# Gate tiles of the second block: the product with the root on VectorE, straight from PSUM

## The reference, cut to what matters

```python
h = rms_norm(x, norm_mix_g[layer])
z = h @ w_in[layer]
y_a = hgrn2_mixer(...)              # from columns of z
y_b = forgetting_attention(...)     # from columns of z
gate_a = jax.nn.sigmoid(z[..., OFF_GATE:OFF_GATE + D_MODEL])
gate_b = jax.nn.sigmoid(z[..., OFF_GATE + D_MODEL:IN_COLS])
merged = gate_a * (y_a @ w_branch_a[layer]) + gate_b * (y_b @ w_branch_b[layer])
x = x + merged @ w_out[layer]
```

## Time and profile before

| | us |
|---|---|
| three timed runs | 1060.25, 1057.53, 1059.84 |
| their median | 1059.84 |
| profiled execution | 1060.18 |
| its span, first to last instruction | 1058.4 |
| TensorE busy | 992.4 (94%) |
| VectorE busy | 702.0 (66%) |
| ScalarE busy | 532.7 (50%) |
| GpSimd busy | 65.6 (6%) |
| mean granted TensorE clock | 0.956 of full |

### The profile page before, as it was taken

One profiled execution on the slowest core, in us unless ns is written; L12 is line 12 of the kernel. 1 busy time (PEld: TensorE's weight loads), 2 busy tenths in 40 slices (PEclk: granted clock), 3 DMA queues, 4 the chain that ended last, 5 costly groups with the idle time before them and its releaser, 6 DMA issues.

```text
span 1058.4 us, 15667 instructions
## 1 busy us (share of the span) xinstructions
PE 992.4 (94%) x6699; PEld 912.0 (86%) x6699; DVE 702.0 (66%) x810; ACT 532.7 (50%) x641; POOL 65.6 (6%) x73
## 2 busy tenths in 40 slices
PE   5999889999978979999999899998999999999988
PEld 4998888989878968989998788898798999999976
DVE  5876693434957487878887659979437555455463
ACT  4555611224474644767776654365354543434352
POOL 3000330410000100000000000002000000000000
PEclk9999997897979879999999999999999999999989
DMA  7655301002224325979999144434235466555521
GB/s 221 218 179 159 96 25 41 1 2 80 81 80 149 129 80 185 356 291 348 360 362 351 53 159 160 125 122 145 87 120 171 159 200 203 193 191 169 199 80 41
DMA packets 91195, 168.54 MB, mean 159 GB/s; under 512 B 6268, under 2 KB 61941, under 8 KB 86262
## 3 DMA queue, kind: packets, MB, share of 16 engines
q1 hardware_dynamic: 90374, 167.22, 46.0%
q10 hardware_dynamic: 752, 0.33, 0.1%
HBM read 166.48 MB, written 1.05 MB: 158 GB/s over the span
## 4 chain that ended last, share of the span: by engine, by line
PE 70%; DVE 15%; ACT 9%; issue 4%; DMA 0%; ACTq 0%; DVEq 0%
PE ps L1004 8%; PE ps L1007 7%; PE ps L1006 7%; PE ps L1022 7%; PE ps L1023 7%; PE ps L1024 7%; DVE w_lo L1740 5%; ACT w_hi L518 4%; PE ps L1394 3%; PE ps L1395 3%; PE ps L1396 3%; PE ps L1218 2%; PE ps L1231 2%; PE ps L1227 2%; PE ps L1434 1%
## 5 line engine op out<-in xcount | busy, mean ns | idle before, releaser
L1740 DVE TENSOR_TENSOR w_lo<-raw,w_hi 128x2048 fp32r<-128x2048 f32 (+1 forms) x158 | 365.6, 2318 | 167.2 <-ACT w_hi L518 166.1
L518 ACT ACTIVATE w_hi<-raw 128x2048 fp32r<-128x2048 f32 (+1 forms) x158 | 299.9, 1902 | 80.6 <-PE ps L1024 63.2
L1004 PE MATMUL ps<-h_hi,w_hi 128*128 128x256 f32 x768 | 222.0, 289 | 3.2 <-DVE h_lo L1750 2.1
L1007 PE MATMUL ps<-h_hi,w_lo 128*128 128x256 f32 x768 | 219.8, 286 | 0.0
L1006 PE MATMUL ps<-h_lo,w_hi 128*128 128x256 f32 x768 | 219.8, 286 | 0.0
L1004 PEld LDWEIGHTS ps<-h_hi,w_hi 128*128 128x128 f32 x768 | 150.2, 196 | 5.3 <-issue 3.5
L1006 PEld LDWEIGHTS ps<-h_lo,w_hi 128*128 128x128 f32 x768 | 150.2, 196 | 0.4
L1007 PEld LDWEIGHTS ps<-h_hi,w_lo 128*128 128x128 f32 x768 | 149.9, 195 | 0.0
L1022 PE MATMUL ps<-w_hi,h_hi 128*128 128x512 f32 (+1 forms) x240 | 95.1, 396 | 2.5 <-DVE h_lo L2094 2.1
L1023 PE MATMUL ps<-w_lo,h_hi 128*128 128x512 f32 (+1 forms) x240 | 93.5, 390 | 0.0
L1024 PE MATMUL ps<-w_hi,h_lo 128*128 128x512 f32 (+1 forms) x240 | 93.1, 388 | 0.0
(11 more groups left out here) (454 smaller groups left out, 1595.9 us busy)
## 6 DMA issues: line engine op xcount, KB each, us to landing
raw<-in_w_in SPq DMA_DIRECT2D x36, 1024.0 KB, 5.1
raw<-in_w_exp_gate SPq DMA_DIRECT2D x20, 1024.0 KB, 5.2
raw<-in_w_exp_up SPq DMA_DIRECT2D x20, 1024.0 KB, 4.9
raw<-in_w_exp_down SPq DMA_DIRECT2D x20, 1024.0 KB, 5.1
raw<-in_w_ffn_gate SPq DMA_DIRECT2D x11, 1024.0 KB, 5.2
raw<-in_w_ffn_up SPq DMA_DIRECT2D x11, 1024.0 KB, 5.3
raw<-in_w_ffn_down SPq DMA_DIRECT2D x11, 1024.0 KB, 4.8
raw<-in_w_out SPq DMA_DIRECT2D x8, 1024.0 KB, 5.0
```

The costliest lines, as they stand in the source:

```text
L518: act.activation(w_hi[:, j % SPL, 0:kt * n], raw[:, j % RAW, 0:kt * n], ACT.Copy).then_inc(w_high, 1)
L1004: pe.matmul(o, hi[:, k, cols], a_hi[:, k, :], start=(k == 0 and (whole or c == 0)), stop=False)
L1007: last_mm = pe.matmul(o, lo[:, k, cols], a_hi[:, k, :], start=False, stop=(k == kt - 1 and (whole or c == len(outs) - 1)))
L1740: dve.tensor_tensor(w_lo[:, j % SPL, 0:kt * n], raw[:, j % RAW, 0:kt * n], w_hi[:, j % SPL, 0:kt * n].bitcast(F32), sub).then_inc(w_ready, 1)
```

## The change

ScalarE no longer copies the gate tiles of the second block and GpSimd no longer multiplies them. VectorE multiplies each tile by `root_rep` as it reads it from the bank, writes it into `gate2` and raises `s_gate_ev2`. ScalarE's sigmoid waits for that semaphore at 8; `s_gate_sc` is gone. ScalarE's `ahead` calls stay where they were, without the copies. TensorE's program is unchanged. The eight products are placed in VectorE's order behind the low parts named in the diff; the second one stands in the middle of `o_norm`. (`gate_out` stays for the first block.)

```diff
@@ gpsimd
-            pool.wait_ge(s_rrep, 1)
-            for c in range(8):
-                pool.wait_ge(s_gate_ev2, c + 1)
-                g = gate2[:, 2 * c:2 * c + 2, :]
-                pool.tensor_tensor(g, g, mid(root_rep, 2), ALU.mult).then_inc(s_gate_sc, 1)
@@ scalar
-            gate_out(GATE2, 0, gate2, s_gate_ev2)
+            ahead(GATE2[1])
             act.wait_ge(s_hg_ps, 3)
             act.activation(ho, split3(bank(2, 2), 2), ACT.Copy).then_inc(s_hg_ev, 1)
-            gate_out(GATE2, 1, gate2, s_gate_ev2)
+            ahead(GATE2[2])
...
-            gate_out(GATE2, 2, gate2, s_gate_ev2)
+            ahead(GATE2[3])
             out_high(1, 2)
-            gate_out(GATE2, 3, gate2, s_gate_ev2)
-            gate_out(GATE2, 4, gate2, s_gate_ev2)
+            ahead(GATE2[4])
+            ahead(GATE2[5])
...
-            gate_out(GATE2, 5, gate2, s_gate_ev2)
-            gate_out(GATE2, 6, gate2, s_gate_ev2)
+            ahead(GATE2[6])
+            ahead(GATE2[7])
             prob_tiles(prob2_t, 6)
-            gate_out(GATE2, 7, gate2, s_gate_ev2)
...
-            act.wait_ge(s_gate_sc, 8)
+            act.wait_ge(s_gate_ev2, 8)
@@ vector
+            def gate_scaled(c):
+
+                dve.wait_ge(w_used, GATE2[c] + 1)
+                dve.tensor_tensor(gate2[:, 2 * c:2 * c + 2, :], split3(bank(6 + c % 2), 2), mid(root_rep, 2),
+                                  mult).then_inc(s_gate_ev2, 1)
...
             ahead(GATE2[1])
+            gate_scaled(0)
+            def gate_two():
+                ahead(GATE2[2])
+                gate_scaled(1)
+
             o_norm(ho, hsq, 1, HG_HEADS, HG_D, rep[:, C_ONORM:C_ONORM + HG_D], z2[:, :, Z2_G:Z2_G + 512],
-                   lambda: ahead(GATE2[2]))
+                   gate_two)
...
             ahead(GATE2[3])
+            gate_scaled(2)
             out_low(1, 2)
             ahead(GATE2[4])
+            gate_scaled(3)
             ahead(GATE2[5])
+            gate_scaled(4)
             softmax(prob2, ...
             ahead(GATE2[6])
+            gate_scaled(5)
             ahead(GATE2[7])
+            gate_scaled(6)
             ahead(PROJ2[0][0])
+            gate_scaled(7)
             attention_low(1)
```

More of the change, by code:

```diff
@@ L352, in two_block_program @@
             "first_half_of_down_in_psum", "root_diagonal_ready", "root_rows_in_psum", "root_rows_ready"))
-        s_scaled, s_gate_sc, s_ple_half = (sem(n) for n in (
-            "scaled_by_root", "gate_scaled_by_root", "ple_tile_in_psum"))
+        s_scaled, s_ple_half = (sem(n) for n in (
+            "scaled_by_root", "ple_tile_in_psum"))
         SQUARES = (2, 4, 4, 4, 4, 4)
```

## The result

The change made the kernel slower by a third of a percent. Twelve runs have a median of 1062.25 us, twelve of the kernel before 1058.01; the ratio is 1.0033, 95% interval 1.002 to 1.0047, about +3.5 us. A second comparison on the chip gave 1.0036 (1.0017 to 1.0055). The profiled execution has a span of 1059.6 us.

A forecast was written before the change was run, and what follows sets the result against it. VectorE was taken to bound the chain before 730.3 us, TensorE behind it. VectorE's -1.70 + 0.65 turn TensorE's slack into a stall: +4.5 at the logits, -0.5 at tile 6, +4.0 in all; 1064.0 us, range 1060.8 to 1066.6.

The forecast's parts named there:

- its own case: Late first product stalls TensorE before chunk 2 with slow clock behind; 1062.6 to 1065.7 us, chance 0.65.
- slower by over 0.3%: Outcome class for the whole kernel: a time above 1063.0 us, given chance 0.64.
- Item 2: Cost of each bank-times-root product on VectorE: 0.65 us, between 0.63 and 0.69.
- Item 3: Silent GpSimd gives VectorE's head norms back 1.70 us of lengthened instructions; bounds 0 and 1.70.
- Item 4: TensorE before chunk 2: waits for tile 0's product, starting at 720.56 instead of 713.82, 6.7 us idle.
- Item 5: TensorE from chunk 2 to logits: 4.6 us slow clock costing 2.0, bounds 1.3 and 2.6; logits +4.5.
- Item 6: VectorE behind the first product: output norm and later products off the path; tightest is product 2, margin 1.6 us.
- Item 7: ScalarE loses eight copies of 0.6 us; only tile 6's is on the chain, so -0.5 us.
- The sum at the sigmoid: Net of all terms: +4.5 at the logits, -0.5 at tile 6, nothing later taking time back: +4.0 us.
- C: Rival: slow clock behind the chunk 2 pause lasts 9 us, costing 3.9 instead of 2.0: 1066.1; chance 0.08.
- D: Rival: clock stays full in the pause before chunk 2, so the wait costs its length alone: 1062.2; chance 0.08.
- Rival B: VectorE stays the bound up to the output transposes, making the change worth -0.9 us: 1059.3; chance 0.07.

## Why the prediction was right

Forecast 1064.0 (range 1060.8 to 1066.6), slower; measured 1062.25 against 1058.01, +3.5 by the ratio, where +4.0 was the sum. The mechanism came as described: product late, TensorE idle, slow clock behind it. The 1.75 us between the two times come from the base: the forecast stood on three runs of before with a median of 1059.84, twelve have 1058.01. For that reason 1062.25 lies just below 1062.6, where the prediction let its own case begin. (Its two margins, 0.7 and 0.6 with 1 us each, give 1062.3 to 1065.6, and the chances of "slower by over 0.3%" add up to 0.655; neither slip matters.)

- *Item 2, the product:* 0.65 forecast, 0.61 of the chain (0.68 long).
- *Item 3, GpSimd:* -1.70 forecast. From the mark to the end of the low part of chunk 3 before has 16.89 us, after 15.20: -1.69. Shown by the kernel without products, and by the one that moves them. The lock of the Trainium skill (SBUF — State Buffer, Who interferes with whom) is in line with it: the rows that grow by 1.1 us in the kernel with late products both read two SBUF tensors. That the lock is the cause, no run shows. In the trace before, GpSimd is lengthened too. Its product at 711.47 starts inside the low part shown here and takes 1.94 us; the one at 715.69 starts ahead of the gain product at 715.88 and takes 1.32.

  ```profile
  710.00 2.28 DVE L1740 TENSOR_TENSOR w_lo<-raw,w_hi 128x2048 fp32r<-128x2048 f32 x1
  ```
- *Item 4, the stall:* chunk 2 forecast 15.88 us from the mark, measured 15.86; pause 6.7 forecast, 6.48 measured. Shown by the runs that move the product: no pause there with an early one, 11.26 us with a later one.
- *Item 5, the slow clock:* forecast 4.6 us, cost 2.0; measured 6.1, 5.0 and 6.05, the cost 2.7 in chunk 2 of the first profile. This term was mis-sized by up to 0.7: the length reached its upper bound of 6.1, the cost stood 0.1 above its bound of 2.6. In front of chunk 4 the slow clock fell away, worth 1.35 by forecast; the window went from 8.24 to 6.56. From the start of chunk 2 to the logits 22.6 were forecast and 22.75, 22.27 and 22.76 measured, so part of the mis-sized cost was made up elsewhere. The logits: +4.5 forecast; +4.68, +4.20 and +4.70 in the three profiles.
- *Item 6, the cover:* product 1 ended at 723.65, asked for at 728.75. Product 2 ended 1.1 us ahead of chunk 4's start in the first profile, 1.6 forecast: the thinnest cover, as named. That the number was near is in part luck: the four terms that the prediction lists behind 730.4 add up to 737.2, not 735.7, and would leave 0.1. The copies of q and k start at 727.48, beside the transposes and not behind their end at 728.75, and that is where the cover comes from. `attention_low` ended at 787.84, some 2.9 us early.
- *Item 7, tile 6:* -0.5 forecast. Chunk 6's end to chunk 7's start went from 4.17 to 3.74: -0.43. In the kernel before and the two that keep the copy (without products, and with late ones) TensorE's pause there is 1.32 us; wherever ScalarE no longer makes it, 0.89 or 0.90.
- *The sum at the sigmoid:* +4.0 forecast; +4.27, +3.78 and +4.29.

Rivals C and D are out by the change's own profiles: the slow clock lasted 5.0 to 6.1 us, not 9, and it was there. Even behind the pause of 11.26 us it lasted 4.6.

Rival B named a wrong price. It set the state with an early first product at 0.9 us faster and looked no further than the stall that it removed; the run with products 0 and 1 forward is 3.7 us slower than before, since tile 2 is the next one late. The 1.6 us of cover that item 6 gives it exist only because the stall at chunk 2 makes TensorE late. All three products have to move before the price holds (0.8 measured).

## What to carry to other kernels

An instruction that frees a buffer for the bottleneck engine belongs where that engine asks for it; whether it costs 0.6 us on one engine or 1.9 us on two others matters less than what it is queued behind. When a wait is taken out of the plan, walk on along the same semaphore: each later count has its own time of asking, and a cover that was computed behind a stall goes with the stall. Count a quiet engine as an engine that may be slowing another: here GpSimd at 6% of the span cost VectorE's chain 1.7 us, and the clock 1.3 more.

## What was not expected of the hardware

The slow clock behind a pause does not follow the pause's length: 6.48, 6.12 and 6.47 us of idle were followed by 6.1, 5.0 and 6.05 us of work at 1.2 GHz, 11.26 by 4.6 and 3.98 by 4.4. A pause of 1.37 us (three kernels) left the clock at 2.4 GHz, and so did one of 2.23 for the 1.09 us of transposes behind it; behind one of 2.56 it fell. The slow clock thus cost the same program 2.2 to 2.7 us in chunk 2, from one execution to the next. The execution with the shorter slow stretch also kept the full clock for more of its pause: the mean granted clock in the pause is 0.85 there and 0.68 in the other two. Why, no run shows.

```profile
712.60:718.72 6.12, 0.00 (x1) 0.85 0.41 144
```
